# A second buffer for the sample values, raw w_out blocks in the space of the gate tiles, the w_out split shared with GpSimd, and sample jobs between the thirds of the last gate tile

## The chip, the cores and the metric

The kernel runs on one core of one Trainium2 chip. The metric is the device time of one execution in microseconds (us). The kernel before takes 933.46 us (median of 3 runs, 929.93 to 934.06).

## The reference, cut to what matters

One inference step of a one-layer decoder, for a prompt of 1024 tokens and for 8 sample sequences with one new token each and 512 past tokens in a paged cache (pages of 128 tokens).

```python
hn = rms_norm(x, g_n)
p  = hn @ w_in                  # 3344 columns: q, k, v of every group, and the gate path z
o_a = fox_attention(...)        # 4 heads, cumulative log-forget bias
o_b = nsa_attention(...)        # compressed blocks (64 tokens @ w1, w2), selected blocks, window
o_c = pool_mix(...)             # trailing means, per-group linear map
o_m = mem_attention(...)        # 256 memory tokens
y  = x + (concat[o_a, o_b, o_c, o_m] * silu(z)) @ w_out     # w_out 1024 x 1024
y  = rms_norm(y, final_g)
```

For the samples the past keys and values come page by page from `cache_fox_kv` and `cache_nsa_kv` by `page_table`, and from `state_nsa_win` and `cache_mem_kv`. Everything is float32.

## The kernel before, in words

**Engines and queues.** Five instruction streams are written out by hand and linked by semaphores: `pe` (TensorE), `act` (ScalarE), `dve` (VectorE), `pool` (GpSimd), `sp` (SyncE). Four of them walk the same list `STEPS`. Nearly all DMAs are issued by `sp`, in the order written, and a wait in that stream holds everything behind it. A page is found with `page(i)`, a load of a table entry into a register of `sp`.

**Products in two parts.** A float32 product is made of three passes (`passes`, L500 to L502): hi by hi, hi by lo and lo by hi, where hi is the operand rounded to fp32r and lo the rest. The projection weights come in 31 tiles of 128 columns (`TILES`); `pool` splits each one from `WR` into `WH` and `WL` (L1827, L1829), and `project(m)` multiplies it with the normalised tokens `hh`, `hl` (1032 columns: 1024 prompt tokens and 8 samples) in three thirds of 344.

**Compression.** `load_pair(q)` brings half of what a sample's page pair needs (32 values of q). For each of its two pages it issues one DMA for each of two heads g, 256 contiguous bytes at a time (L1937). `pair_job(n, kind)` on TensorE turns the four tiles of sample n with transposes (L658), and ScalarE or VectorE copies the result to `FT`. `compress(kind)` multiplies `FT` with `w1` in four quarters (L676); each quarter is a DMA of 1 MB (`load_w1`, L1944) into one of two halves of `PP`. On `sp` these DMAs stand among the pair loads: the fourth quarter of kind 0 is behind the loads of q = 23 and 24.

**Sample keys and values.** `sample_keys` runs four gate tiles in thirds and turns and scores the keys of one sample between thirds (L802, L811 to L817). It ends with small products for the new keys (L836 to L843). `sample_values` runs the last gate tile in three thirds (`project_chunk`), then turns the probabilities `X` (L854 to L858), then the pooled sums (L863), then multiplies these with the pool map (L869).

**Output product.** `mix` takes nine row tiles t: eight of 128 prompt rows and t = 8 with the 8 samples. Each has two halves of 512 columns, eight steps of k and three passes: 48 matmuls of 512 columns. From t = 1 on, `values(b)` stands ahead of a tile (L886): 14 products of the probabilities of sample b with its values. t = 1 has `values(0)` and `values(1)` ahead of it, t = 2 to 7 one sample each. Values are in the single ring `v_ring` (`XT` and three parts of `PP`), so the loads of sample b + 1 wait for the products of sample b (`load_values`, counted by `s_vr`).

**The raw w_out.** It comes in eight blocks of 128 columns (`load_wo`, L2118) into four places, two in `WR` and two in `PP`. ScalarE makes the hi part of each (`out_hi`) into the space of `hh`, VectorE the lo part (`out_lo`, L1487) into that of `hl`. Blocks 4 to 7 are loaded when the lo part of blocks 0 to 3 is done. Because the blocks overwrite columns of `hh`, block 0 and 1 can be written after the first third of the last gate tile, blocks 2 to 4 after the second, blocks 5 to 7 after the last.

**Gates.** `gate_product(n)` (L1473) multiplies the attention output by the tile `AUG[:, j]` of silu(z) and counts `s_zo`; after it that tile is only needed for the 8 sample columns. `gate_hi(t)` and `gate_lo(t)` split the product for a row tile. At the end of a row tile VectorE adds the input rows (L1798), ScalarE squares and takes the root, VectorE scales (L1777), and `sp` stores.

Of the kernel before, what the change touches and what calls it, by code (L numbers as in the profile page):

```python
# [21 lines left out]
F32 = mybir.dt.float32  # L22
# [7 lines left out]
P = 128  # L30
# [3 lines left out]
NB = 8  # L34
# [119 lines left out]
def build(nc, x_p, x_s, c_fox, c_lf, c_nsa, st_win, st_pool, c_mem, ptab, mem_p, norm_g, w_in, b_f, pe_, w1,  # L154
# [3 lines left out]
    with ExitStack() as ctx:  # L158
# [65 lines left out]
        gg = NAT[:, 0:KC * NB].rearrange("p (k b) -> p k b", k=KC)  # L224
# [45 lines left out]
        def pair_slot(q):  # L270
# [8 lines left out]
            return where.rearrange("p (a c) -> p a c", a=2)  # L279
# [63 lines left out]
        s_wo = [sem(f"s_wo{i}") for i in range(4)]  # L343
        s_woh = sem("s_woh")
        s_wol = sem("s_wol")
        s_eva = sem("s_eva")
# [37 lines left out]
        s_kv = [sem(f"s_kv{i}") for i in range(4)]  # L384
        s_lfp = sem("s_lfp")
# [60 lines left out]
        v_ring = [XT[:, 0:1024], PP[:, 2048:2560], PP[:, 2560:3072], PP[:, 3072:3584]]  # L446
        XW = WR[:, :, :, :].rearrange("p s k c -> p s (k c)")

        def wo_raw(j):

            if j % 4 < 2:
                return WR[:, (NT + j) % 2, :, :]
            return PP[:, (j % 2) * 1024:(j % 2 + 1) * 1024].rearrange("p (k c) -> p k c", k=KC)
# [6 lines left out]
        def _(pe):  # L460
# [386 lines left out]
            def sample_values():  # L847
                project_chunk(NT - 1, 0)
                project_chunk(NT - 1, 1)
                project_chunk(NT - 1, 2)  # L850
                pe.wait_ge(s_px, 1)
                out = job_a()
                for pg in range(NPG):
                    last = tr(out[:, pg * P:(pg + 1) * P], X[:, pg * P:(pg + 1) * P], ident[:, :])  # L854
                last.then_inc(s_TA, 1)
                out = job_d()
                tr(out[0:NB, 0:P], XN8[:, :], ident[:, :])
                tr(out[0:NB * SCB, P:P + 32], XC[0:32, 16:16 + NB * SCB], ident[0:32, 0:32]).then_inc(s_TD, 1)  # L858

# [4 lines left out]
                last.then_inc(s_TA, 1)  # L864
                jobs_taken()
# [5 lines left out]
                last.then_inc(s_TD, 1)  # L871

            def values(b):
# [6 lines left out]
                for pg in range(NPG):  # L880
                    for br, width, npg in ((0, 256, NPG), (1, P, NPG), (2, P, NPG), (3, 256, 2)):
                        if pg == 0:
                            pe.wait_ge(s_kv[br], (64 if br in (0, 1) else 16) * (NB + b + 1))
                        if pg >= npg:
                            continue
                        last = mm(PS[32 * br:32 * br + 32, 6 + p % 2, b % 2 * 256:b % 2 * 256 + width],  # L886
                                  PTs[:, pg, 32 * br:32 * br + 32], v_ring[br][:, pg * width:(pg + 1) * width],
# [1315 lines left out]
```

## Time and profile before

| | |
|---|---|
| time, median of 3 runs | 933.46 us (929.93 to 934.06) |
| time of the profiled execution | 932.5 us |
| its span, first to last instruction | 930.8 us |
| TensorE matmul busy | 826.7 us, 89% |
| VectorE, ScalarE, GpSimd busy | 42%, 29%, 16% |
| mean granted TensorE clock | 0.946 of full speed |

A line of the profile gives source line, engine, operation, names of output and inputs, and times in us. "SPq" is a DMA issue on SyncE. "PEclk" is the granted TensorE clock, 1.00 being 2.4 GHz and 0.50 being 1.2 GHz. A matmul is recorded longer than the step from one to the next, since consecutive ones overlap. An idle time is put down to whatever ended it.

### The profile page before, as it was taken

How to read it: one execution, taken by the hardware profiler on the slowest of the kernel's cores; microseconds unless marked ns; L12 is line 12 of the kernel's file. 1: busy time of each engine (PE TensorE's matmuls, PEld its weight loads, DVE VectorE, ACT ScalarE, POOL GpSimd, SP SyncE). 2: the span in 40 equal slices, each digit the busy share in tenths (PEclk: the TensorE clock that was granted, in tenths of full speed). 3: DMA queues.
4: the chain of work that ended last, by engine and by line, in shares of the span. 5: the costliest groups of instructions: out<-in, count | busy, mean ns of one | idle time of the engine just before them, and what ended most of it. 6: DMA issues, size and time to landing. Idle time of an engine off the chain costs nothing.

```text
span 930.8 us, 15434 instructions
## 1 busy us (share of the span) xinstructions
PE 826.7 (89%) x5755; PEld 679.0 (73%) x5755; DVE 395.4 (42%) x765; ACT 268.1 (29%) x624; POOL 146.2 (16%) x104
## 2 busy tenths in 40 slices
PE   3788998797999978899989999988999999799997
PEld 3788687794666978798956666668988788567773
DVE  3731734114565111206426777855833125433333
ACT  4612720103444102202125444631022224221111
POOL 4745001331000201103101000003231110000000
PEclk9979999897999989999799999989999999889999
DMA  7510002235321334040022000010135447365631
GB/s 227 171 49 24 1 22 47 57 77 156 105 113 30 103 103 133 21 136 23 14 84 62 2 1 2 1 26 25 47 87 159 146 134 193 93 198 186 204 103 49
DMA packets 110409, 79.45 MB, mean 85 GB/s; under 512 B 27237, under 2 KB 104308, under 8 KB 110264
## 3 DMA queue, kind: packets, MB, share of 16 engines
q1 hardware_dynamic: 108880, 77.66, 27.9%
q10 hardware_dynamic: 1456, 0.82, 0.4%
q8 instruction: 46, 0.75, 0.3%
q14 instruction: 27, 0.22, 0.1%
HBM read 68.81 MB, written 13.85 MB: 89 GB/s over the span
## 4 chain that ended last, share of the span: by engine, by line
PE 73%; DVE 10%; ACT 4%; issue 4%; DMA 4%; SPq 3%; POOL 1%; DVEq 0%; ACTq 0%; POOLq 0%
PE PS L500 14%; PE PS L502 14%; PE PS L501 14%; PE PS L582 6%; PE PS L628 5%; PE PS L607 4%; PE PS L676 3%; PE PS L802 2%; PE PS L886 2%; PE PS L592 2%; DVE AUG L1417 1%; DVE stat L1367 1%; PE PS L632 1%; DMA PP<-in_nsa_w 1%; PE PS L595 1%
## 5 line engine op out<-in xcount | busy, mean ns | idle before, releaser
L500 PE MATMUL PS<-HH,WH 128*128 128x344 f32 (+3 forms) x824 | 285.6, 347 | 7.2 <-issue 2.9
L501 PE MATMUL PS<-HL,WH 128*128 128x344 f32 (+3 forms) x824 | 280.1, 340 | 0.0
L502 PE MATMUL PS<-HH,WL 128*128 128x344 f32 (+3 forms) x824 | 279.8, 340 | 0.0
L500 PEld LDWEIGHTS PS<-HH,WH 128*128 128x128 f32 (+1 forms) x824 | 160.0, 194 | 21.4 <-issue 8.3
L501 PEld LDWEIGHTS PS<-HL,WH 128*128 128x128 f32 (+1 forms) x824 | 159.8, 194 | 7.9
L502 PEld LDWEIGHTS PS<-HH,WL 128*128 128x128 f32 (+1 forms) x824 | 159.5, 194 | 8.2
L1827 POOL TENSOR_TENSOR WH<-WR,onesc 128x1024 fp32r<-128x1024 f32 x31 | 61.3, 1977 | 604.2 <-PE PS L502 237.1
L1124 ACT ACTIVATE PP<-PS,stat 128x640 f32<-128x640 f32 (+7 forms) x96 | 67.8, 710 | 102.9 <-DVE stat L1367 102.9
L1367 DVE TENSOR_REDUCE stat<-PS 128x1 f32<-128x640 f32 (+7 forms) x96 | 65.1, 720 | 60.1 <-PE PS L595 59.7
L1829 POOL TENSOR_TENSOR WL<-WR,WH 128x1024 fp32r<-128x1024 f32 x31 | 78.2, 2522 | 2.4
L607 PE MATMUL PS<-ident,PP 128*128 128x128 f32 x472 | 67.6, 281 | 9.5 <-DVE AUG L1417 6.9
L607 PEld LDWEIGHTS PS<-ident,PP 128*128 128x128 f32 x472 | 54.9, 143 | 15.6 <-DVE AUG L1417 13.0
L582 PE MATMUL PS<-AUG 64*128 64x512 f32 (+3 forms) x288 | 59.9, 522 | 2.0 <-issue 2.0
L1417 DVE COPY AUG<-PS 128x512 f32<-128x512 f32 (+3 forms) x80 | 48.9, 628 | 8.3 <-PE PS L607 7.3
L628 PE MATMUL PS<-AUG,NAT 128*64 128x128 f32 (+1 forms) x640 | 47.2, 289 | 4.4 <-ACT AUG L1016 2.8
L676 PE MATMUL PS<-OB,PP 128*128 128x161 f32 x256 | 41.1, 326 | 10.2 <-DMA PP<-in_nsa_w 5.4
L676 PEld LDWEIGHTS PS<-OB,PP 128*128 128x128 f32 x256 | 39.9, 211 | 11.1 <-DMA PP<-in_nsa_w 6.1
L628 PEld LDWEIGHTS PS<-AUG,NAT 128*64 128x64 f32 x640 | 35.4, 136 | 11.2 <-DVE AUG L1417 4.2
L1016 ACT ACTIVATE AUG<-PS 128x128 f32<-128x128 f32 (+5 forms) x88 | 40.9, 465 | 7.7 <-PE PS L607 7.2
L1338 DVE COPY VS<-PS 64x8 f32<-64x8 f32 x8 | 1.4, 169 | 96.8 <-PE PS L502 96.8
L582 PEld LDWEIGHTS PS<-AUG 64*128 64x128 f32 x288 | 25.0, 193 | 22.0 <-issue 18.7
L1798 DVE TENSOR_TENSOR PP<-PS,WR 128x1024 f32<-128x1024 f32 (+1 forms) x9 | 11.0, 1223 | 66.3 <-PE PS L502 45.1
(322 smaller groups left out, 862.8 us busy)
## 6 DMA issues: line engine op xcount, KB each, us to landing
WR<-in_w_in SPq DMA_DIRECT2D x26, 512.0 KB, 4.3
PP<-in_nsa_w SPq DMA_DIRECT2D x8, 1024.0 KB, 6.1
OB<-in_x_prompt SPq DMA_DIRECT2D x8, 512.0 KB, 6.0
out<-NAT SPq DMA_DIRECT2D x2, 2048.0 KB, 7.8
PP<-in_cache_fox_kv SPq DMA_DIRECT2D x32, 128.0 KB, 2.3
PP<-in_cache_nsa_kv SPq DMA_DIRECT2D x64, 64.0 KB, 1.9
PP<-in_state_nsa_win SPq DMA_DIRECT2D x16, 256.0 KB, 3.0
PP<-in_cache_mem_kv SPq DMA_DIRECT2D x16, 256.0 KB, 3.2
```

The costliest lines, as they stand in the source:

```text
L500: mm(out, lhs[0], rhs[0], start=(k == 0), stop=False)
L501: mm(out, lhs[0], rhs[1], start=False, stop=False)
L502: return mm(out, lhs[1], rhs[0], start=False, stop=(k == KC - 1))
L582: mm(bk(score_bank(u, e) + c // 4)[:, 0:n * P], q[r, i * P:(i + 1) * P], k[r, (k0 + c) * P:(k0 + c + n) * P], start=True, stop=False)
L607: last = tr(bk(4 + g % 3)[:, (b - c) * P:(b - c + 1) * P], PP[:, p0:p0 + P], ident[:, :])
L628: mm(bk(7)[e * DH:(e + 1) * DH, 0:wide * P], v, p_, start=(b == 0), stop=(b == (1 if what == "mem" else nk - 1)))
L676: last = mm(bk(e)[:, 0:R_ALL + 1], w1s[:, n % 2, jj, e * P:(e + 1) * P], FT[:, j, :], start=(j == 0), stop=(j == NJ - 1))
L1124: last = act1(PP[:, c:c + nk * P], flat(score_bank(u, e), nk), ACT.Exp, bias=stat[:, k:k + 1], accum_out=stat[:, 16 + k:17 + k])
L1367: v.tensor_reduce(stat[:, k:k + 1], flat(score_bank(u, e), nk), AX.X, ALU.max, negate=True).then_inc(s_nm, 1)
L1417: v.tensor_copy(turned_p(u - 1, e, c, n), bk(4 + g % 3)[:, 0:n * P]).then_inc(s_cD, 1)
L1827: g.tensor_tensor(hi_, WR[:, s, :, :], ones, ALU.mult).then_inc(s_wcp, 1)
L1829: g.tensor_tensor(lo_, WR[:, s, :, :], hi_.bitcast(F32), ALU.subtract).then_inc(s_split, 1)
```

## The change

- **Pair loads.** Each page is fetched with one DMA for both heads (512 contiguous bytes), 64 issues instead of 128. `pair_job` makes eight matmuls with 64 weight columns, into one or the other half of the PSUM partitions, in place of four 128 x 128 transposes.
- **Values.** Two rings: even samples in `NAT` and `PP`, odd ones in the tiles `AUG[:, 0]` to `AUG[:, 2]`. Sample 1 is loaded first, then w_out blocks 0, 4, 5, 6, 2, 3, then three branches of sample 0, then blocks 1 and 7, then the last branch of sample 0.
- **w_out.** Blocks 4 to 7 go to `AUG[:, 3]` to `AUG[:, 6]` and wait only for a gate product. `pool` splits blocks 1, 3 and 5 with two tensor_tensor each; ScalarE and VectorE split the other five. The first half of row tile 0 waits for two blocks of each, the second half for all.
- **Order.** The pooled sums and the pool map stand ahead of the first and second third of the last gate tile, the probabilities between the second and the last. The copy of the pool map's result on VectorE stands ahead of the scaling of the probabilities.
- **Row tile 8.** hi and lo of the samples stand side by side in one weight tile (columns 0 to 7 and 32 to 39), so two matmuls do the work of three: 32 instead of 48. VectorE then adds two parts.

```diff
@@ pair_job (TensorE), load_pair (SyncE)
-                pe.wait_ge(s_pair[n], 128 * (kind + 1))
+                pe.wait_ge(s_pair[n], 64 * (kind + 1))
-                        last = tr(out[:, (2 * g + a) * P:(2 * g + a + 1) * P],
-                                  pair_slot(q)[:, g, :], ident[:, :])
+                        for r in range(2):
+                            last = mm(out[r * DH:(r + 1) * DH, (2 * g + a) * P:(2 * g + a + 1) * P],
+                                      pair_slot(q)[:, r, g * DH:(g + 1) * DH], ident[:, :], start=True, stop=True)
...
-                    for g in range(2):
-                        src = c_nsa[0, bass.ds(pg, 1), :, kind, g, :].rearrange("o (j r) d -> (o j) r d", r=2)
-                        sp.dma_start(dst, src).then_inc(s_pair[n], 16)
+                    src = c_nsa[0, bass.ds(pg, 1), :, kind, :, :].rearrange("o (j r) g d -> (o j) r (g d)", r=2)
+                    sp.dma_start(pair_slot(q)[a * DH:(a + 1) * DH], src).then_inc(s_pair[n], 16)
@@ places
-        v_ring = [XT[:, 0:1024], PP[:, 2048:2560], PP[:, 2560:3072], PP[:, 3072:3584]]
+        v_rings = [[NAT[:, 1024:2048], PP[:, 2048:2560], PP[:, 2560:3072], PP[:, 3072:3584]],
+                   [AUG[:, 0, 0:1024], AUG[:, 1, 0:512], AUG[:, 1, 512:1024], AUG[:, 2, 0:512]]]
...
+            return AUG[:, j - 1, 0:1024].rearrange("p (k c) -> p k c", k=KC)
+
+        WO_POOL = (1, 3, 5)
+        WO_CHUNK = (0, 0, 1, 1, 1, 2, 2, 2)
@@ mix (TensorE)
+                    if t == NQ:
+                        for half in range(2):
+                            for k in range(KC):
+                                c = slice(half * 512, (half + 1) * 512)
+                                both = TH[:, 1024 + k * P:1024 + k * P + 32 + NB]
+                                rest = both[:, 0:NB], wol[:, CHUNK[k], c]
...
-                            pe.wait_ge(s_wol, KC // 2 * (half + 1))
+                            pe.wait_ge(s_wol, 2 if half == 0 else 5)
+                            pe.wait_ge(s_wop, 2 if half == 0 else 3)
@@ end of the GpSimd stream
+            for n, j in enumerate(WO_POOL):
+                c = slice(j * P, (j + 1) * P)
+                pool.wait_ge(s_wo[j], 16)
+                if WO_CHUNK[j] < 2:
+                    pool.wait_ge(s_zp, 2 * (NT - 1 - ZK) + WO_CHUNK[j] + 1)
+                else:
+                    pool.wait_ge(s_proj, NT)
+                g.tensor_tensor(woh[:, :, c], wo_raw(j), ones, ALU.mult).then_inc(s_wph, 1)
+                pool.wait_ge(s_wph, n + 1)
+                g.tensor_tensor(wol[:, :, c], wo_raw(j), woh[:, :, c].bitcast(F32), ALU.subtract).then_inc(s_wop, 1)
@@ SyncE
-                    sp.wait_ge(s_wol, j - 3)
+                    sp.wait_ge(s_zo, j)
...
+            first = pages(1)
+            sp.wait_ge(s_zo, 3)
+            for br in range(4):
+                load_value(1, br, first)
             first = pages(0)
             load_wo(0)
+            for j in (4, 5, 6):
+                load_wo(j)
             load_wo(2)
             load_wo(3)
             for br in (1, 2, 3):
...
             load_wo(1)
+            load_wo(7)
-            sp.wait_ge(s_sx, 1)
-            load_kv(0, 0, 1, first, v_ring)
+            sp.wait_ge(s_sS, NB)
+            load_value(0, 0, first)
...
-                    sp.wait_ge(s_vr, 4 * (b - 1) + (2, 3, 4, 1)[br])
-                    load_kv(b, br, 1, pn, v_ring)
+                    sp.wait_ge(s_vr, 4 * (b - 2) + (2, 3, 4, 1)[br])
+                    load_value(b, br, pn)
@@ end of row tile 8 (VectorE)
+                            link(v.tensor_tensor(y1, y2[0:NB], XW[0:NB, s, :], ALU.add))
+                            last = v.tensor_tensor(y1, y2[32:32 + NB], y1, ALU.add)
```

## Rows read from the trace of the kernel before

**Rows 1.** The page: busy time of the engines, then two of its costliest groups
```profile
PE 826.7 (89%) x5755; PEld 679.0 (73%) x5755; DVE 395.4 (42%) x765; ACT 268.1 (29%) x624; POOL 146.2 (16%) x104
...
L1827 POOL TENSOR_TENSOR WH<-WR,onesc 128x1024 fp32r<-128x1024 f32 x31 | 61.3, 1977 | 604.2 <-PE PS L502 237.1
...
L1798 DVE TENSOR_TENSOR PP<-PS,WR 128x1024 f32<-128x1024 f32 (+1 forms) x9 | 11.0, 1223 | 66.3 <-PE PS L502 45.1
```
**Rows 2.** Waits of TensorE, whole span: sum, times, longest
```profile
PE PS L676 <- DMA PP<-in_nsa_w: 5.4, 3, 2.0
...
PE PS L500 <- POOL WL L1829: 2.2, 1, 2.2
```
**Rows 3.** Timeline, SyncE and TensorE, pairs of kind 0: start, duration
```profile
161.40 11.50 SPq L1937 DMA_DIRECT2D PP<-in_cache_nsa_kv  x12
...
170.57 1.09 PE L658 MATMUL PS<-ident,PP 128*128 128x128 f32 x4 [5.32 <-DMA PP<-in_cache_nsa_kv]
```
**Rows 4.** Timeline, SyncE and TensorE, compression of kind 0
```profile
336.49 7.44 SPq L1937 DMA_DIRECT2D NAT<-in_cache_nsa_kv  x8
343.98 0.59 SPq L1944 DMA_DIRECT2D PP<-in_nsa_w  x1
...
341.70 6.33 PE L676 MATMUL PS<-OB,PP 128*128 128x161 f32 x32 [2.00 <-DMA PP<-in_nsa_w]
350.00 4.65 PE L676 MATMUL PS<-OB,PP 128*128 128x161 f32 x32 [1.98 <-DMA PP<-in_nsa_w]
```
**Rows 5.** Windows: PE, PEld, DVE, ACT, POOL busy, PEclk, DMA share, GB/s
```profile
794.00:796.00 2.00, 1.69 (x10) 1.40 (x9) 1.21 (x6) 1.16 (x2) 0.00 (x0) 0.50 1.20 295
...
916.00:924.00 8.00, 8.00 (x36) 3.01 (x34) 1.40 (x2) 0.00 (x0) 0.00 (x0) 1.00 0.16 66
```
**Rows 6.** Timeline of TensorE from the last gate tile to row tile 1
```profile
788.91 0.60 PE L854 MATMUL PS<-ident,OB 128*128 128x128 f32 x4
...
794.64 0.77 PE L500 MATMUL PS<-HH,WH 128*128 128x512 f32 x1 [0.31 <-issue]
...
808.45 0.40 PE L886 MATMUL PS<-XT,NAT 128*32 128x256 f32 x1
...
820.81 0.50 PE L500 MATMUL PS<-HH,WH 128*128 128x512 f32 x1
```
**Rows 7.** Timeline of SyncE's DMA issues around w_out and the values
```profile
764.88 0.45 SPq L2108 DMA_DIRECT2D out<-OB  x1
768.22 0.39 SPq L2118 DMA_DIRECT2D WR<-in_w_out  x1
...
810.55 1.96 SPq L2059 DMA_DIRECT2D XT<-in_cache_fox_kv  x4
...
815.10 0.51 SPq L2065 DMA_DIRECT2D PP<-in_cache_mem_kv  x1
```
**Rows 8.** Timeline of ScalarE: hi parts of two w_out blocks as they land
```profile
794.09 1.06 ACT L1016 ACTIVATE HH<-WR 128x1024 fp32r<-128x1024 f32 x1 [1.10 <-DMA WR<-in_w_out]
...
797.67 1.06 ACT L1016 ACTIVATE HH<-PP 128x1024 fp32r<-128x1024 f32 x1 [0.71 <-DMA PP<-in_w_out]
```
**Rows 9.** DMA issues from 740 us on: count, KB, median us to landing
```profile
WR<-in_w_out SPq DMA_DIRECT2D x4, 512.0 KB, 4.5
```
**Rows 10.** Timelines of GpSimd and VectorE where both have two SBUF inputs
```profile
637.23 2.40 POOL L1829 TENSOR_TENSOR WL<-WR,WH 128x1024 fp32r<-128x1024 f32 x1
...
650.73 3.43 POOL L1829 TENSOR_TENSOR WL<-WR,WH 128x1024 fp32r<-128x1024 f32 x1
...
637.40 3.32 DVE L1430 TENSOR_TENSOR NAT<-PP 128x1038 f32<-128x1038 f32 x1
640.75 1.23 DVE L1430 TENSOR_TENSOR PP<-NAT 64x1036 f32<-64x1036 f32 x1
```
**Rows 11.** The chain that ended last: start, duration, matmuls of 64 and 32 columns
```profile
238.12 1.90 PE PS L628 x32
...
832.24 1.84 PE PS L886 x22
```

More of the change, by code:

```diff
@@ L342, in build @@
         s_zt = sem("s_zt")
-        s_wo = [sem(f"s_wo{i}") for i in range(4)]
+        s_wo = [sem(f"s_wo{i}") for i in range(KC)]
         s_woh = sem("s_woh")
         s_wol = sem("s_wol")
+        s_wop = sem("s_wop")
+        s_wph = sem("s_wph")
         s_eva = sem("s_eva")
@@ L384, in build @@
         s_kv = [sem(f"s_kv{i}") for i in range(4)]
+        s_kvo = [sem(f"s_kvo{i}") for i in range(4)]
         s_lfp = sem("s_lfp")
@@ L871, in sample_values @@
                 last.then_inc(s_TD, 1)
+                project_chunk(NT - 1, 1)
+                pe.wait_ge(s_px, 1)
+                out = job_a()
+                for pg in range(NPG):
+                    last = tr(out[:, pg * P:(pg + 1) * P], X[:, pg * P:(pg + 1) * P], ident[:, :])
+                last.then_inc(s_TA, 1)
+                mark["X"] = nA[0]
+                out = job_d()
+                tr(out[0:NB, 0:P], XN8[:, :], ident[:, :])
+                tr(out[0:NB * SCB, P:P + 32], XC[0:32, 16:16 + NB * SCB], ident[0:32, 0:32]).then_inc(s_TD, 1)
+                project_chunk(NT - 1, 2)
             def values(b):
@@ L919, in mix @@
                     s = t % 2
+                    if t == NQ:
[4 more added lines that the diff above has]
+                                rest = both[:, 0:NB], wol[:, CHUNK[k], c]
+                                if k == KC - 1:
+                                    mm(bk(half)[0:NB, :], *rest, start=False, stop=False)
+                                last = mm(bk(half)[0:32 + NB, :], both, woh[:, CHUNK[k], c], start=(k == 0),
+                                          stop=(k == KC - 1))
+                                if k < KC - 1:
+                                    mm(bk(half)[0:NB, :], *rest, start=False, stop=False)
+                        last.then_inc(s_y, 1)
+                        continue
                     for half in range(2):
                         if t == 0:
-                            pe.wait_ge(s_wol, KC // 2 * (half + 1))
+                            pe.wait_ge(s_wol, 2 if half == 0 else 5)
+                            pe.wait_ge(s_wop, 2 if half == 0 else 3)
                         if t == NB - 1 and half == 1:
@@ L927, in mix @@
                             c = slice(half * 512, (half + 1) * 512)
-                            out = bk(2 * s + half)[0:P if t < NQ else NB, :]
-                            last = passes(out, g, (woh[:, CHUNK[k], c], wol[:, CHUNK[k], c]), k)
+                            last = passes(bk(2 * s + half), g, (woh[:, CHUNK[k], c], wol[:, CHUNK[k], c]), k)
                     last.then_inc(s_y, 1)
@@ L1233, in _ @@
                 elif step == "sample_values":
-                    take_chunk(NT - 1, 0)
+                    out = job()
+                    done(copy(PLT.rearrange("p j b -> p (j b)"), out[:, 0:2 * NB]))
                     act.wait_ge(s_sx, 1)
@@ L1716, in _ @@
                     v.tensor_reduce(XC[0:32, 4:5], XC[0:32, 8:16], AX.X, ALU.max, negate=True).then_inc(s_sx, 1)
+                    out = job()
+                    done(v.tensor_copy(oTs[:, 6:8, :], out[:, 0:2 * NB].rearrange("p (j b) -> p j b", j=2)))
                     dve.wait_ge(s_se, 1)
@@ L1736, in _ @@
                     done(v.tensor_copy(PTc, out[0:NB * SCB, P:P + 32]))
-                    out = job()
-                    done(v.tensor_copy(oTs[:, 6:8, :], out[:, 0:2 * NB].rearrange("p (j b) -> p j b", j=2)))
+                    out_lo(4, 3)
+                    gate_product(9)
+                    out_lo(6, 4)
+                    out_lo(7, 5)
+                    gate_lo(1)
+                    dve.wait_ge(s_fA, mark["X"])
+                    dve.wait_ge(s_fD, nD[0])
                     for i in (6, 7):
@@ L2072, in _ @@
             for br in range(4):
[L2073 removed]
+                load_kv(0, br, 0, first, k_ring, s_kv)
             sp.wait_ge(s_lfr, 1)
@@ L2126, in _ @@
                     slot_read(NB - 1, max(br, 2))
-                load_kv(0, br, 1, first, v_ring)
+                load_value(0, br, first)
             load_wo(1)
-            sp.wait_ge(s_sx, 1)
-            load_kv(0, 0, 1, first, v_ring)
+            load_wo(7)
+            sp.wait_ge(s_sS, NB)
+            load_value(0, 0, first)
+            sp.wait_ge(s_sS, NB + 1)
             sp.dma_start(gf, fin_g.rearrange("(o d) -> o d", o=1).partition_broadcast(P)).then_inc(s_gf, 16)
-            for j in range(4, KC):
-                load_wo(j)
             def load_values(b):
```

109 lines of the change are left out of this document (52 added, 57 removed).

## The prediction

> **What bounds the kernel now.** First the page: TensorE is busy 89% of the span and no other engine half of it [rows 1]. So the path is TensorE's own list, and the change can gain in two ways only: fewer matmuls, or shorter holes between them. The waits of TensorE by what ended them come next [rows 2]. Two kinds are touched by the edits: waits for compression weights and cached pages, and one for a split by GpSimd. The timelines of SyncE and TensorE say why these came late [rows 3, 4]. Last come the stretch from the last gate tile to row tile 1 [rows 6] and the windows [rows 5]. The reader should see two holes there. Between the turned probabilities (788.91) and the first matmul of row tile 0 (794.64) only small sample jobs run, and the granted clock then is 0.50, that is 1.2 GHz; row tile 0 takes 808.45 - 794.64 = 13.81 us. Between 808.45 and 820.81 there are 12.36 us for two samples' values, whose products take 1.84 us each where nothing is late [rows 11]. The second sample's loads are issued at 810.55, when the ring is free [rows 7].
>
> **Pair loads.** TensorE first. Eight matmuls of 64 columns replace four transposes of 128. At full clock 32 such matmuls take 1.90 us [rows 11], so eight take 0.48; the four transposes took 1.09 at half clock [rows 3], 0.54 at full. I count nothing; with 16 jobs the ends are -1 and +1 us. Then SyncE. Four page look-ups fill the time from 764.88 + 0.45 to 768.22, 0.72 us each [rows 7]. Twelve issues with five look-ups between them took 11.50 [rows 3], so an issue costs (11.50 - 3.60) / 12 = 0.66. Half of the issues go.
>
> In kind 0 the job at 170.57 waited 5.32 us for q = 5, whose last issue stood behind seven issues and three look-ups: 161.40 + 6.78 = 168.2, so 2.4 us to land. Now three issues and three look-ups stand ahead: 161.40 + 4.14 + 2.4 = 167.9, 2.6 us sooner. The start at 161.40 hangs on a VectorE result (SyncE copies the forget biases just ahead) and stays. The wait of 2.2 us for GpSimd [rows 2] lies before it, on a weight load behind 16 pair issues, and should go too; but TensorE then only reaches the same late pages earlier. So the two together give 2.6, not 4.9.
>
> In compression the fourth quarter's weights were issued at 343.98 behind eight pair issues and waited for until 350.00 [rows 4], 6.0 us later. Four issues less (2.64) bring them at 347.4; TensorE is ready at 348.0, so the wait of 1.98 goes. The slot for them was free at 339.7, before the third quarter began to wait, and holds nothing back. The other waits in this group end with loads that wait for TensorE itself. **Sum: -4.6 us**; bounds -6 (clock regained as well) and 0 (if issue time per page grows with the wider rows).
>
> **w_out, values and the order of jobs.** The pooled sums and the map now precede the last gate tile's second third, so TensorE would be ready for row tile 0 at about 791 to 792, against 794.64. I ask when the split blocks are ready. SyncE is free at 765.3. It now looks up sample 1's pages (2.9, to 768.2), issues its ten loads (810.55 to 815.61 in rows 7, so 5.1, to 773.3), looks up sample 0's pages (2.9, to 776.2), and only then issues block 0, which went at 768.22 before. A block lands 4.5 us after its issue [rows 9], so block 0 at 780.7, early enough. But all the transfers now stand in one row. Blocks 5 and 7 landed so close behind each other that two blocks need 797.67 - 794.09 = 3.58 us, 1.79 each [rows 8], at the 295 GB/s of the window [rows 5]. Block 1 is the seventh block: six steps, 10.7 us, and 768 KB of values of sample 0 ahead of it, 2.7 us at the same rate. It lands at 780.7 + 13.4 = 794.1.
>
> GpSimd takes block 1 first. A block costs it 1.98 [rows 1] + 2.40 [rows 10] + small gaps, 4.4 us, so blocks 1 and 3 would be done at 802.9. Now the rows on sharing: VectorE's op at 637.40 took 3.32 instead of 1.23 and ended 1.1 us after GpSimd's, which began first; GpSimd's at 650.73 took 3.43 instead of 2.40 [rows 10]. The two take turns where both read two SBUF tensors. VectorE has lo parts of blocks 6 and 7 and of row tile 1 to do in just this stretch; I let two of the three fall into GpSimd's chain, at 1.03 each: 805.0 (bounds 802.9 and 806.0).
>
> The Trainium skill says the same against the change: GPSIMD Engine Reference, section Specifications, has the SBUF interfaces shared with VectorE, with contention where VectorE's instruction has two SBUF inputs. By it the sum would be that of 805 or 806, without it that of 803; the trace agrees, with 3.43 against 2.40 us.
>
> So row tile 0 starts at 805.0, 10.4 us later than before. What is queued behind: TensorE's whole mix, hence every later evict and store. GpSimd's third block ends at 809.5 to 811; the first half of tile 0 lasts from 805 to about 813 at its old speed, so that wait is hidden, and costs what it exceeds 813. Tile 0 takes the old 13.81 us, half clock at its head included: 818.8. All values are there by then (the last transfer, sample 0's fox part, lands near 798), so two samples take 3.7 us and 0.1: 822.6 against 820.81. **Sum: +1.8 us.** The hole of the values is filled, but its time has been moved to the front of row tile 0. Later samples are already hidden behind 11 us of matmuls in each tile and gain nothing. The eight small stores and the input rows follow on SyncE by about 798; the rows land before 806, long before 818.8 where VectorE wants them.
>
> **Row tile 8.** 36 matmuls start in 8.00 us [rows 5], 0.22 each; 16 less save 3.6. They end the kernel's list, so all of it is on the path. VectorE pays one more operation over 1024 columns behind them, 1.22 [rows 1] and a gap. **Sum: -2.35 us.** What comes next there, the store of tile 7 and the input row of the samples, is done by then.
>
> **Total:** -4.6 + 1.8 - 2.35 = -5.2 us. Against the profiled execution (932.5) that is 927.3; the median of the runs is 0.96 above it, 928.3. I take 928.
>
> **Rivals.** About 0.5% (4.7 us) is what a measurement of this kernel tells from no change: 928.8 and 938.1 are the bounds.
>
> 1. *The blocks come in time.* If block 1 landed by the end of the first third (782) and block 3's split needed only the second third (786.5), GpSimd would be done at 791, and the tile would start at 792 without a clock loss: 48 x 0.22 = 10.7 us, then 3.8: 806.5 against 820.8, -14 in place of +1.8, in all 911 to 912. For it: SyncE could be faster than its look-ups in rows 7 say, and the wait there may hide another cause. Against it: 3.9 MB between blocks 0 and 1 at 295 GB/s. Halfway cases lie at 917 to 924. Chance 0.2 for the two.
> 2. *The early gains are not kept, or GpSimd is later still.* If the wider pair loads cost SyncE more each, or all three VectorE operations and more meet GpSimd, then the total is between -3 and +4: 930 to 937. For it: each term rests on a difference of 2 to 3 us against landing times that vary as much. Chance 0.18.
> 3. *Slower, by one mechanism: the row of transfers.* The blocks and values between (3.9 MB) take 13.4 us at the rate of rows 5 and 8. A us more is a us on the path, so from 10.8 us more, a row 1.8 times as slow (163 GB/s), the total passes 938.1; at twice the time it is 927.3 + 13.4, 940.7. For it: six blocks in one row were never seen in this trace, only four at a time, and small pages are mixed in. Against it: the window that was full moved 295 GB/s. Chance 0.12.
> 4. *The second ring does nothing, all values were hidden anyway:* excluded by 12.36 us in rows 6 against 3.7.
>
> My forecast (924 to 932) has chance 0.5, of which 0.3 below 928.8. Faster: 0.3 + 0.2 = 0.5. Same: 0.2 + 0.18 = 0.38. Slower: 0.12. For 8 in 10 the range goes down into the halfway cases, 917, and up to 936; the likeliest case's own is 924 to 932.
>
> **What the changed profile would show.** The pair job near 170 waits under 5 us and its end comes at 168; no wait for weights at compression's fourth quarter. The first w_out issue is near 775 less the early gain, and TensorE stands idle some 13 us before row tile 0, released by GpSimd's lo part of block 3; GpSimd's first of six operations is released by a DMA. Between row tiles 0 and 1 there are 4 us, not 12. Row tile 8 takes 7.5 us, with two VectorE operations behind it. I am wrong if TensorE's wait before row tile 0 is short (blocks come faster than one in 1.79 us, or issued earlier), or if it is ended by VectorE or ScalarE; and if the pair jobs show issues longer than 0.66 us or matmuls slower than 0.06 each.

## The result and the profile after

| | before | after |
|---|---|---|
| median of 20 runs each | 931.69 us (926.35 to 939.45) | 925.52 us (920.54 to 930.92) |
| ratio, 95% interval | | 0.9932 (0.9911 to 0.9953) |
| profiled execution, its span | 932.5, 930.8 us | 924.19, 922.4 us |
| mean granted TensorE clock | 0.946 | 0.959 |

The change gains 0.7%, about 6.2 us of 931.7. The two profiled executions differ by 8.4 us. To see where, I cut both at starts of the same GpSimd instructions (the split of a projection tile, `WH<-WR`) and at the first matmuls of row tiles 0 and 1. Every run below is cut in the same way; no times of different kernels are compared on one clock. Line numbers are some 10 to 50 higher in the kernel after (L668 is the old L658, L686 the old L676, L509 to L511 the old L500 to L502).

| stretch, us | before | after | difference |
|---|---|---|---|
| start to the split at 89.85 | 89.85 | 89.69 | -0.2 |
| kind 0 pair loads and attention, to 311.87 | 222.02 | 218.07 | -3.9 |
| compression of kind 0, to 366.11 | 54.24 | 52.62 | -1.6 |
| kind 1 pair jobs, to 423.37 | 57.26 | 58.55 | +1.3 |
| code that no edit touches, to the last projection split (751.36) | 327.99 | 325.74 | -2.3 |
| from it to row tile 1 (820.81) | 69.45 | 70.26 | +0.8 |
| row tile 1 to the end of the span | 109.99 | 107.47 | -2.5 |

The fifth line is the one to distrust: nothing there was edited. Over all ten kernels profiled in this case the same code takes 324.5 to 333.9 us there, and its length follows the granted clock of the stretch: 324.5 to 326.2 us at a mean of 0.97 (three profiles, that of the kernel after among them), 328.0 to 329.7 at 0.96 (five, that of the kernel before among them), 332.3 and 333.9 at 0.95. So the profiled pair overstates the gain by some 2 us, and what remains, 6.1, is close to the 6.2 of the medians.

The page of the kernel after, engines' busy time; [rows 1] has the same line of before:

```profile
PE 815.7 (88%) x5931; PEld 674.2 (73%) x5931; DVE 396.2 (43%) x763; ACT 265.7 (29%) x621; POOL 160.9 (17%) x110
```

Waits of TensorE in the kernel after, by what ended them (sum, times, longest); compare [rows 2]:

```profile
PE PS L503 <- DVE OB L1324: 15.3, 7, 6.4
PE PS L509 <- POOL HL L1936: 15.0, 1, 15.0
...
PE PS L686 <- DMA PP<-in_nsa_w: 5.2, 3, 2.2
...
PE PS L668 <- DMA PP<-in_cache_nsa_kv: 4.1, 1, 4.1
```

One wait of 15.0 us for GpSimd is new, the longest of the kernel; the waits of compression for weights have hardly moved (5.4 to 5.2). Timelines of TensorE, kernel after: the late pair job and compression's third and fourth quarters ([rows 3, 4]), then the last third, row tile 0 and row tile 1 ([rows 6]):

```profile
166.62 1.97 PE L668 MATMUL PS<-ident,PP 128*64 128x128 f32 x16 [4.13 <-DMA PP<-in_cache_nsa_kv]
...
337.41 4.65 PE L686 MATMUL PS<-OB,PP 128*128 128x161 f32 x32 [1.60 <-DMA PP<-in_nsa_w]
344.27 4.65 PE L686 MATMUL PS<-OB,PP 128*128 128x161 f32 x32 [2.21 <-DMA PP<-in_nsa_w]
...
781.97 0.32 PE L511 MATMUL PS<-HH,WL 128*128 128x344 f32 x1
797.33 0.77 PE L509 MATMUL PS<-HH,WH 128*128 128x512 f32 x1 [15.04 <-POOL HL L1936]
...
811.36 0.40 PE L900 MATMUL PS<-NAT 128*32 128x256 f32 x1
...
814.93 0.50 PE L509 MATMUL PS<-HH,WH 128*128 128x512 f32 x1
```

The sample jobs no longer stand between the last third and row tile 0, and the products of two samples now take 814.93 - 811.36 = 3.57 us where they took 12.36. But in front of row tile 0 TensorE has nothing to do for 15 us. SyncE's issues and GpSimd's timeline say why:

```profile
757.38 0.44 SPq L2154 DMA_DIRECT2D out<-OB  x1
760.50 3.00 SPq L2105 DMA_DIRECT2D AUG<-in_cache_fox_kv  x4
...
768.84 0.37 SPq L2164 DMA_DIRECT2D WR<-in_w_out  x1
...
781.39 0.47 SPq L2164 DMA_DIRECT2D WR<-in_w_out  x1
```

```profile
786.75 1.89 POOL L1934 TENSOR_TENSOR HH<-WR,onesc 128x1024 fp32r<-128x1024 f32 x1 [37.71 <-DMA WR<-in_w_out]
788.73 2.35 POOL L1936 TENSOR_TENSOR HL<-WR,HH 128x1024 fp32r<-128x1024 f32 x1
791.03 2.87 POOL L1934 TENSOR_TENSOR HH<-PP,onesc 128x1024 fp32r<-128x1024 f32 x1
793.98 3.20 POOL L1936 TENSOR_TENSOR HL<-PP,HH 128x1024 fp32r<-128x1024 f32 x1
```

Block 0 of w_out is issued at 768.84, 11.0 us after SyncE was done with the store at 757.38 + 0.44; block 1 is issued at 781.39 and has landed at 786.75, 17.9 us behind block 0's issue. GpSimd needs 10.4 us for blocks 1 and 3, and its last two operations are longer than the 1.98 and 2.40 of [rows 1, 10]. Windows of the row of transfers, of the hole and of row tile 0, kernel after (columns as in [rows 5]):

```profile
769.00:787.00 18.00, 13.29 (x93) 12.45 (x90) 11.62 (x26) 10.56 (x16) 0.25 (x1) 0.98 0.98 276
```

```profile
782.00:797.00 15.00, 0.29 (x2) 0.00 (x1) 10.44 (x12) 4.29 (x6) 10.09 (x4) 0.64 0.78 248
797.00:804.00 7.00, 6.67 (x17) 5.31 (x18) 0.00 (x0) 0.00 (x0) 4.42 (x3) 0.55 0.00 0
804.00:811.00 7.00, 7.00 (x31) 5.65 (x31) 0.00 (x0) 0.00 (x0) 0.00 (x0) 1.00 0.01 2
```

From block 0's issue until block 1 is there the DMA engines are busy 98% of the time, so the transfers themselves are the row. The granted clock is at its lower level (1.2 GHz, 0.50) for most of the first six microseconds of row tile 0, as it was before; so the hole costs its own length and, behind it, a slow start of the tile. VectorE after the last row tile, kernel after:

```profile
914.73 1.21 DVE L1835 TENSOR_TENSOR PP<-PS,WR 8x1024 f32<-8x1024 f32 x1 [3.18 <-PE PS L941]
915.98 1.22 DVE L1836 TENSOR_TENSOR PP<-PS,PP 8x1024 f32<-8x1024 f32 x1
```

Row tile 8's first matmul starts at 907.11 and the sum can start at 914.73: 7.6 us.

### The profile page after: what moved, and what is told of

It reads as the page before. It is cut to its first block, busy times and chain, and to the rows that moved or that the text cites. A ratio compares the mean times of both kernels' runs of the same rounds, so it can differ in the third digit from the quotient of the medians.

```text
span 922.4 us, 15598 instructions
## 1 busy us (share of the span) xinstructions
PE 815.7 (88%) x5931; PEld 674.2 (73%) x5931; DVE 396.2 (43%) x763; ACT 265.7 (29%) x621; POOL 160.9 (17%) x110
## 4 chain that ended last, share of the span: by engine, by line
PE 71%; DVE 9%; SPq 5%; issue 4%; DMA 4%; ACT 4%; POOL 2%; DVEq 0%; POOLq 0%; ACTq 0%
PE PS L509 14%; PE PS L511 13%; PE PS L510 13%; PE PS L591 6%; PE PS L637 5%; PE PS L616 4%; PE PS L686 3%; PE PS L601 2%; SPq L2105 2%; PE PS L900 2%; DVE AUG L1445 1%; PE PS L812 1%; DVE stat L1395 1%; DMA PP<-in_nsa_w 1%; PE PS L668 1%
## 5 line engine op out<-in xcount | busy, mean ns | idle before, releaser
L509 PE MATMUL PS<-HH,WH 128*128 128x344 f32 (+2 forms) x808 | 276.7, 342 | 19.7 <-POOL HL L1936 15.0
L510 PE MATMUL PS<-HL,WH 128*128 128x344 f32 (+2 forms) x808 | 271.4, 336 | 0.0
L511 PE MATMUL PS<-HH,WL 128*128 128x344 f32 (+2 forms) x808 | 271.1, 335 | 0.0
L509 PEld LDWEIGHTS PS<-HH,WH 128*128 128x128 f32 x808 | 156.2, 193 | 32.2 <-issue 23.7
L511 PEld LDWEIGHTS PS<-HH,WL 128*128 128x128 f32 x808 | 156.1, 193 | 6.0
L510 PEld LDWEIGHTS PS<-HL,WH 128*128 128x128 f32 x808 | 156.3, 193 | 5.7
L686 PE MATMUL PS<-OB,PP 128*128 128x161 f32 x256 | 40.0, 320 | 9.8 <-DMA PP<-in_nsa_w 5.2
L686 PEld LDWEIGHTS PS<-OB,PP 128*128 128x128 f32 x256 | 38.8, 205 | 10.7 <-DMA PP<-in_nsa_w 6.0
L1285 ACT ACTIVATE WR<-PP 128x1024 f32<-128x1024 f32 (+1 forms) x9 | 9.5, 1058 | 100.5 <-DVE PP L1831 93.3
```

The lines of the kernel that those rows point to most:

```text
L509: mm(out, lhs[0], rhs[0], start=(k == 0), stop=False)
L510: mm(out, lhs[0], rhs[1], start=False, stop=False)
L511: return mm(out, lhs[1], rhs[0], start=False, stop=(k == KC - 1))
L686: last = mm(bk(e)[:, 0:R_ALL + 1], w1s[:, n % 2, jj, e * P:(e + 1) * P], FT[:, j, :], start=(j == 0), stop=(j == NJ - 1))
```

## Experiments

The kernel before ran beside each: 932.67 us (median of 35 runs) beside the first four experiments, which have 12 runs each, 932.14 us (11 runs) beside the last four, which have 6 runs each. So kernels of different groups are best compared by their ratios. "Hole" is the idle time of TensorE right before row tile 0. The last two columns count from the last projection split on GpSimd.

| kernel | median us | ratio to before (95%) | hole | row tile 0 starts | end |
|---|---|---|---|---|---|
| before, profiled | 931.69 | 1 | 0.3 | 43.3 | 179.4 |
| after, profiled | 925.52 | 0.9932 (0.9911 to 0.9953) | 15.0 | 52.7 | 177.7 |
| pair loads and matmuls alone | 925.82 | 0.9922 (0.9892 to 0.9951) | as before | 43.1 | 179.7 |
| eight matmuls alone | 934.91 | 0.9999 (0.9971 to 1.0026) | as before | 41.4 | 177.4 |
| row tile 8 alone | 930.92 | 0.9962 (0.9932 to 0.9991) | as before | 41.6 | 175.5 |
| sample 1's values late | 930.2 | 0.9967 (0.9935 to 0.9998) | 8.6 | 46.3 | 181.4 |
| block 1 second | 920.77 | 0.9873 (0.9831 to 0.9916) | 0.6 | 44.8 | 170.7 |
| all blocks first | 915.38 | 0.9855 (0.9803 to 0.9906) | 0.6 | 47.9 | 171.2 |
| no GpSimd | 916.59 | 0.9835 (0.9789 to 0.9881) | 5.7 | 44.9 | 169.0 |
| blocks first, no GpSimd | 911.63 | 0.9774 (0.9730 to 0.9817) | 0.6 | 39.7 | 162.2 |

### 1. Pair loads and their matmuls alone

```diff
-                pe.wait_ge(s_pair[n], 128 * (kind + 1))
+                pe.wait_ge(s_pair[n], 64 * (kind + 1))
...
-                        last = tr(out[:, (2 * g + a) * P:(2 * g + a + 1) * P], pair_slot(q)[:, g, :], ident[:, :])
+                        for r in range(2):
+                            last = mm(out[r * DH:(r + 1) * DH, (2 * g + a) * P:(2 * g + a + 1) * P],
+                                      pair_slot(q)[:, r, g * DH:(g + 1) * DH], ident[:, :], start=True, stop=True)
...
-                        src = c_nsa[0, bass.ds(pg, 1), :, kind, g, :].rearrange("o (j r) d -> (o j) r d", r=2)
...
+                    src = c_nsa[0, bass.ds(pg, 1), :, kind, :, :].rearrange("o (j r) g d -> (o j) r (g d)", r=2)
...
```

> The kernel before with the pair part alone: one DMA per page for both heads, and eight matmuls of 64 weight columns per pair job. Theory A, the prediction's: fewer issues bring two late loads sooner, -4.6 us at the start of the attention of the second phase and after compression of kind 0, and the eight matmuls cost nothing; -4.6 us in all. Theory B, from the profile after: a pair job now shows 1.09 us at full clock and 1.97 at half, where it showed 0.60 and 1.09, so 16 jobs cost 16 x 0.45 = 7 us more of TensorE, of which some lies in waits that shrink; then the part is worth between 0 and +3 us of loss, or less gain than 2 us.

Measured: 925.82 us, ratio 0.9922 (0.9892 to 0.9951). The interval is -4.6 to -10 us and excludes that the early gain is lost. In the profiles, the time from the split at 89.85 to that at 423.37 is 333.5, 333.6 and 334.2 us in the three kernels with narrow loads, and 327.5 to 329.6 in the seven with wide ones, mean 329.1, against 333.8: **-4.7 us**, with -3.6 in kind 0, -2.8 in compression and +1.6 in the kind 1 jobs. The +1.6 is a cost of the eight matmuls, as experiment 2 shows.

### 2. The eight matmuls alone, loads as before

```diff
-                        last = tr(out[:, (2 * g + a) * P:(2 * g + a + 1) * P], pair_slot(q)[:, g, :], ident[:, :])
+                        for r in range(2):
+                            last = mm(out[r * DH:(r + 1) * DH, (2 * g + a) * P:(2 * g + a + 1) * P],
+                                      pair_slot(q)[:, g, r * DH:(r + 1) * DH], ident[:, :], start=True, stop=True)
```

> The kernel before with its narrow loads (two DMAs per page), but eight matmuls of 64 weight columns per pair job in place of four transposes. Theory A: matmuls into two halves of the partitions overlap as in the attention's products, no change (within 1 us). Theory B: 0.45 us more per job, 16 jobs, less what the job waiting for a DMA hides: +5 to +7 us.

Measured: 934.91 us, ratio 0.9999 (0.9971 to 1.0026): no cost that the medians can tell (the interval is -2.7 to +2.4 us). Yet the operation is not the one that I had costed. Two jobs of kind 1, kernel with the eight matmuls alone, timeline of TensorE:

```profile
369.12 1.97 PE L659 MATMUL PS<-ident,VW 128*64 128x128 f32 x32 [1.06 <-ACT KCs L1017]
371.42 1.97 PE L659 MATMUL PS<-ident,NAT 128*64 128x128 f32 x32 [0.34 <-ACT OB L1017]
```

and the same place in the kernel before:

```profile
367.67 1.09 PE L658 MATMUL PS<-ident,VW 128*128 128x128 f32 x8 [1.06 <-ACT KCs L1016]
369.50 1.57 PE L658 MATMUL PS<-ident,NAT 128*128 128x128 f32 x8 [0.74 <-ACT OB L1016]
```

Each line covers two jobs, so 16 of the new matmuls leave 32 records. Each leaves two. The page confirms it: 5931 - 5755 = 176 records more = 16 jobs x (16 - 4) - 16 in row tile 8. It is not the 64 columns: compression issues 128 float32 matmuls with 128 weight columns over its two kinds and leaves 256 records (L676 in its page), while a transpose leaves one (64 of them at L658 in the kernel before, 64 records). What changed is that transposes became plain float32 matmuls. Two jobs take 1.97 us in place of 1.09. The second line shows what hides half of it: the wait for ScalarE's copy shrinks from 0.74 to 0.34 us, so from the first line to the second it is 2.30 us instead of 1.83. Sixteen jobs make some 4 us at that rate if none waits for pages or copies.

In kind 1 the profiles show it. TensorE's first two quarters of compression of kind 1, in the kernels of experiment 3 (old transposes), of experiment 2 and in the kernel after:

```profile
391.70 10.68 PE L676 MATMUL PS<-OB,PP 128*128 128x161 f32 x64 [1.15 <-DVE OB L1581]
```

```profile
393.42 9.01 PE L677 MATMUL PS<-OB,PP 128*128 128x161 f32 x64 [1.08 <-DVE OB L1567]
```

```profile
386.24 10.68 PE L686 MATMUL PS<-OB,PP 128*128 128x161 f32 x64 [1.11 <-DVE OB L1593]
```

The split of the projection tile ahead of the jobs starts at 367.90, 367.56 and 360.38 in the three, so compression starts 23.80, 25.86 and 25.86 us behind it. It is 25.9 in all eight kernels with the new matmuls, all at full clock up to there, as that of experiment 3 is; in the kernel before it is 24.96, with the granted clock at 0.50 for a part of the jobs. So the eight jobs of kind 1 cost 2.1 us. The kernel of experiment 2 wins 1.7 back behind them, since it alone has the full clock in the first quarter (the two quarters take 9.01 us in place of 10.68). That is why its whole stretch is no longer than that of the kernel before (56.75 and 57.26), and why the kernels with wide loads and the same matmuls need 58.4.

### 3. The new row tile 8 alone

```diff
+                    if t == NQ:
+                        for half in range(2):
+                            for k in range(KC):
...
+                                both = TH[:, 1024 + k * P:1024 + k * P + 32 + NB]
+                                rest = both[:, 0:NB], wol[:, CHUNK[k], c]
...
+                            link(v.tensor_tensor(y1, y2[0:NB], XW[0:NB, s, :], ALU.add))
+                            last = v.tensor_tensor(y1, y2[32:32 + NB], y1, ALU.add)
...
```

> The kernel before with the new row tile 8 alone (two matmuls in place of three, and two adds on VectorE). Prediction: 16 x 0.23 = 3.6 us less of TensorE at the end of the list, 1.25 us more of VectorE behind it, -2.35 us. Rival: the samples' gate product or the store of tile 7 ends later than row tile 8 now starts or ends, so nothing is gained (0 us). The profile shows the last matmul to the end as 6.9 + 1.25 us if the first holds.

Measured: 930.92 us, ratio 0.9962 (0.9932 to 0.9991), -3.5 us with an interval of -0.8 to -6.3 that holds the -2.35. VectorE after its last scaling of row tile 7, first the kernel with this edit:

```profile
926.02 1.21 DVE L1819 TENSOR_TENSOR PP<-PS,WR 8x1024 f32<-8x1024 f32 x1 [3.18 <-PE PS L928]
927.27 1.22 DVE L1820 TENSOR_TENSOR PP<-PS,PP 8x1024 f32<-8x1024 f32 x1
```

then the kernel before:

```profile
924.31 1.21 DVE L1798 TENSOR_TENSOR PP<-PS,WR 8x1024 f32<-8x1024 f32 x1 [6.88 <-PE PS L502]
```

VectorE waits 3.70 us less and pays 1.25 for the second sum: -2.45. That the profiled span was longer than that of before (933.7) is no cost of the edit: its clock was 0.933, and the untouched stretch alone took 333.9 us.

### 4. The kernel after with sample 1's values loaded late

```diff
-            first = pages(1)
-            sp.wait_ge(s_zo, 3)
-            for br in range(4):
-                load_value(1, br, first)
             first = pages(0)
             load_wo(0)
...
+            pn = pages(1)
+            for br in range(4):
+                sp.wait_ge(s_vr, (2, 3, 4, 1)[br])
+                load_value(1, br, pn)
```

> The kernel after with sample 1's values loaded where the kernel before loads them, after sample 0's products: the second ring is not used for what it is for, and look-ups and ten issues are taken from ahead of w_out. Theory A (the prediction's): the start of row tile 0 is set by the row of transfers and GpSimd behind it, so it comes 8 us sooner (block 0 issued 8 us sooner), and the wait for sample 1's values comes back with 8 to 9 us; the total is that of the kernel after within 1.5 us. Rival: GpSimd alone sets the start (its blocks are slow whatever lands when), then the start does not move, and the total is 8 us above the kernel after.

Measured: 930.2 us, ratio 0.9967 (0.9935 to 0.9998), 3.3 us above the kernel after by the two ratios. GpSimd gets block 1 35.3 us after the last split, 6.8 sooner than in the kernel after, and row tile 0 starts 6.4 sooner. So SyncE's look-ups, issues and the transfer of sample 1 cost 6.4 to 6.8 us of the path where they stand. But the wait behind row tile 0 comes back: from the first product of values (809.68) to row tile 1 (822.55) it is 12.9 us where the kernel after takes 3.6. The balance at row tile 1 is +2.5 us. The expectation, 8 us in front and 8 to 9 behind with a total within 1.5 us, was too high for the front. By the profiles the second ring pays for itself (the intervals of the two ratios overlap), but it gives 6.4 of the 9.3 us back in front of row tile 0.

### 5. Block 1 issued second

```diff
-            for j in (4, 5, 6):
+            for j in (0, 1, 3, 2, 4, 5, 6):
                 load_wo(j)
-            load_wo(2)
-            load_wo(3)
...
-            load_wo(1)
```

> The kernel after with one thing changed: the issue order of the w_out blocks is 0, 1, 3, 2, 4, 5, 6, then the values, then 7. Theory A: the 15.0 us hole ahead of row tile 0 is the row of transfers in front of block 1; block 1 now lands some 12 us sooner, GpSimd starts as soon as the first third is done and ends block 3 about 7.5 us after the second third, so the hole shrinks from 15 to 3 us and the total falls by 11 to 13 us against the kernel after. Rival B: GpSimd is the bound (two blocks of 5.2 us each with VectorE's turns between), with more turns now that VectorE works beside it all the time: the hole shrinks by 5 us or less.

Measured: 920.77 us, ratio 0.9873 (0.9831 to 0.9916). Waits of TensorE, this kernel:

```profile
PE PS L875 <- DVE cs L1754: 3.4, 1, 3.4
...
PE PS L509 <- POOL HL L1936: 3.2, 1, 3.2
```

The 15.0 us are gone; the 3.2 stand in the middle of row tile 0 (at 802.78), where the second half wants GpSimd's third block. Row tile 0 starts 7.8 us sooner, not 15, and by the two ratios the total falls by 5.5 us, where 11 to 13 (or, by the rival, 5 or less) were expected: neither theory had the whole. The last third ends 6.7 us later than in the kernel after. Of that, 3.4 is a new wait in front of it, for VectorE's softmax of the samples, which was in time in the kernel after. The other 3.3 is the granted clock. It is at 0.50 behind that wait, in part of the last third, and in part of the first third, which costs 1.5 us in this kernel and in the three that follow; why it fell there no run shows. The next run shows the cause of the wait best. GpSimd's third block suffers from the other side, timelines of GpSimd and VectorE in this kernel:

```profile
793.34 6.87 POOL L1934 TENSOR_TENSOR HH<-AUG,onesc 128x1024 fp32r<-128x1024 f32 x1 [2.78 <-PE PS L511]
```

```profile
797.25 1.21 DVE L1509 TENSOR_TENSOR WL<-OB,WH 128x1024 fp32r<-128x1024 f32 x1
```

The operation that takes 1.89 us elsewhere took 6.87. VectorE ran five operations with two SBUF inputs back to back, from 793.43 to 797.25 + 1.21 = 798.46, and GpSimd's ended 1.75 us behind the last of them: it was held through all five, though it is recorded as begun before the first.

### 6. All blocks but one ahead of sample 1's values

```diff
+            for j in (0, 1, 4, 5, 6, 3, 2):
+                load_wo(j)
             first = pages(1)
             sp.wait_ge(s_zo, 3)
...
+            load_wo(7)
             first = pages(0)
-            load_wo(0)
-            for j in (4, 5, 6):
-                load_wo(j)
...
```

> The kernel after with SyncE's order 0, 1, 4, 5, 6, 3, 2 of the w_out blocks ahead of the page look-ups and loads of sample 1, then block 7, then sample 0. Theory A: as with block 1 second, -12 us against the kernel after; blocks come even earlier than they can be used, so there is nothing above that, within 2 us; values of both samples land before 793 and are not waited for (needed at about 797). Rival: the values now come late and a wait stands between row tiles 0 and 1 again (some us back).

Measured: 915.38 us, ratio 0.9855 (0.9803 to 0.9906). Against the kernel after that is 7.2 us by the ratios, where 12 were expected; its six runs lie apart (914.2 to 925.0), and the intervals of experiments 5, 6 and 7 overlap, so what follows rests on the profiles. The rival's wait between row tiles 0 and 1 did not come: 3.6 us as in the kernel after. Row tile 0 starts later than with experiment 5 (47.9 against 44.8). GpSimd, then VectorE, in this kernel:

```profile
772.38 1.90 POOL L1934 TENSOR_TENSOR HH<-WR,onesc 128x1024 fp32r<-128x1024 f32 x1 [26.01 <-PE PS L511]
774.35 2.39 POOL L1936 TENSOR_TENSOR HL<-WR,HH 128x1024 fp32r<-128x1024 f32 x1
776.69 2.07 POOL L1934 TENSOR_TENSOR HH<-PP,onesc 128x1024 fp32r<-128x1024 f32 x1
778.85 2.34 POOL L1936 TENSOR_TENSOR HL<-PP,HH 128x1024 fp32r<-128x1024 f32 x1
```

```profile
772.86 1.43 DVE L1748 TENSOR_TENSOR cs<-cs,GC 128x1 f32<-128x1 f32 x1
774.32 2.70 DVE L1749 TENSOR_SCALAR OB<-OB,cs 128x513 f32<-128x513 f32 x1
777.06 1.74 DVE L1750 TENSOR_SCALAR cs<-E,OB 128x8 f32<-128x8 f32 x1
...
778.89 2.31 DVE L1752 TENSOR_TENSOR cs<-cs,GC 32x1 f32<-32x1 f32 x1
```

and the same four operations of VectorE in the kernel after, where GpSimd is idle:

```profile
773.99 0.16 DVE L1748 TENSOR_TENSOR cs<-cs,GC 128x1 f32<-128x1 f32 x1
774.18 0.49 DVE L1749 TENSOR_SCALAR OB<-OB,cs 128x513 f32<-128x513 f32 x1
774.71 0.23 DVE L1750 TENSOR_SCALAR cs<-E,OB 128x8 f32<-128x8 f32 x1
...
775.03 0.15 DVE L1752 TENSOR_TENSOR cs<-cs,GC 32x1 f32<-32x1 f32 x1
```

Four operations of 1.03 us together take 8.18. Read the ends: each ends within 0.3 us of the GpSimd operation beside it (774.29 and 774.28, 777.02 and 776.74, 778.80 and 778.76, 781.20 and 781.19). A column of one element waits as long as a tile of 1024. TensorE waits 5.2 us for the result, and then runs the last third (783.20 to 789.36) at a mean granted clock of 0.62.

The Trainium skill (GPSIMD Engine Reference, section Specifications) has the SBUF interfaces shared with VectorE, with contention where VectorE's instruction is in a 2-port performance mode or has two SBUF inputs. The trace agrees for the two inputs; that two TENSOR_SCALARs here wait as well would come under the other half of that rule, if they run in such a mode, which no row here names.

### 7. The transfers of the kernel after, GpSimd left out of the split

```diff
-            for n, j in enumerate(WO_POOL):
...
-                g.tensor_tensor(woh[:, :, c], wo_raw(j), ones, ALU.mult).then_inc(s_wph, 1)
...
+                    out_hi(3)
+                    for j in (5, 6, 1, 7):
+                        out_hi(j)
...
-                            pe.wait_ge(s_wol, 2 if half == 0 else 5)
-                            pe.wait_ge(s_wop, 2 if half == 0 else 3)
+                            pe.wait_ge(s_wol, 7 if half == 0 else 8)
...
```

ScalarE makes all eight hi parts and VectorE all eight lo parts; block 1 is the seventh of them, so the first half of row tile 0 waits for seven lo parts.

> The kernel after with its order of transfers, but ScalarE and VectorE split all eight blocks (in the order 0, 2, 4, 3, 5, 6, 1, 7). Theory A, the row of transfers: block 1 still lands at 786.7 (in the profile's time), its hi and lo parts take 2.3 us, so row tile 0 starts at about 789 in place of 797.3: -8 us. So of the hole of 15 us, GpSimd's two blocks are 10.6 and the transfers 4.4 to 7. Rival: VectorE and ScalarE become the bound (eight blocks of 1.1 us each and gates), start not before 793, -4 us.

Measured: 916.59 us, ratio 0.9835 (0.9789 to 0.9881). Waits of TensorE, this kernel:

```profile
PE PS L509 <- DVE HL L1515: 5.7, 1, 5.7
```

The order of the transfers is that of the kernel after, and block 1 lands at the same place, 42.1 us after the last split. Yet of the hole of 15.0 us only 5.7 is left. **GpSimd's share of it is about 9 us, the row of transfers' about 6** (by the start of row tile 0 it is 7.8 and, down to experiment 8, 5.2, since the last third ends 1.5 us later in both, by the slow first third that experiment 5 has too). ScalarE and VectorE split a block in 1.06 and 1.2 us in two steps that overlap from block to block, where GpSimd takes over 4 for each, one after the other.

### 8. Both: blocks first, GpSimd left out

The edits of 6 and 7 together, blocks 5, 6 and 7 split last.

> The kernel after with all w_out blocks but 7 issued ahead of the values, and ScalarE and VectorE splitting all eight in the order of their numbers, no work on GpSimd. Theory A: no transfer and no shared interface is left; row tile 0 starts about 1 us after the last third (783 in the profile's time), -14 us against the kernel after, 1 to 2 us better than with GpSimd. Rival: VectorE's eight lo parts are too slow between the thirds, so that sharing with GpSimd pays (this one 2 us or more slower than all blocks first with GpSimd).

Measured: **911.63 us, ratio 0.9774 (0.9730 to 0.9817)**, 20.5 us below the kernel before and 13.9 below the kernel after (21.1 and 14.7 by the ratios). Row tile 0 of this kernel, timeline of TensorE, and a window around it:

```profile
788.86 0.50 PE L509 MATMUL PS<-HH,WH 128*128 128x512 f32 x1 [0.55 <-ACT AUG L1123]
```

```profile
787.00:800.00 13.00, 12.45 (x57) 9.96 (x55) 8.71 (x14) 4.72 (x6) 0.00 (x0) 1.00 0.65 211
```

The wait left is the one for the last tile's silu. Against the kernel after, row tile 0 starts 12.9 us sooner, and it takes 11.4 us rather than 14.0, since without a hole the granted clock stays at 1.00. The two make 15.5, and the whole from the last split to the end is 15.6 us shorter.

## Why the prediction was right

The forecast was 928, with -5.2 us as the sum; the medians give -6.2, the profile without its untouched stretch -6.1. It was right in its total and near in every term, but several of its reasons were not, and in the pair loads errors of opposite sign cancel. Step by step:

- **Pair loads, -4.6: measured -4.3 in the profiled pair, -4.7 over all profiles.** That the sum is so close is luck: kind 0 and compression gave 1.8 more than their 4.6 over all profiles, and the kind 1 jobs took 1.6 of it back. In kind 0 I had 2.6 and the stretch gave 3.9. The late job's wait ended at 166.62, not at 167.9. Six issues with five look-ups took 7.20 us (160.15 to 167.35), near the 7.56 of my 0.66 and 0.72; what I missed lies ahead of them. I wrote that SyncE's start at 161.40 "stays"; it came 1.25 us sooner. VectorE's scaling of the forget biases, one step of that chain, ran beside a GpSimd lo part in the kernel before (149.38 to 151.73; first row below, kernel before) and alone in the kernel after, where that split had begun at 140.60 (second row), 1.05 us for the one operation:

```profile
150.54 1.73 DVE L1554 TENSOR_SCALAR OB<-OB 4x1024 f32<-4x1024 f32 x1
```

```profile
150.35 0.68 DVE L1581 TENSOR_SCALAR OB<-OB 4x1024 f32<-4x1024 f32 x1
```

- **Compression, -2.0 as a wait that goes: measured -1.6, and the wait did not go.** The fourth quarter's issue did move, from 2.3 us behind the start of the third quarter's matmuls to 0.1 behind it (337.54 against 337.41). But the transfer landed 6.7 us after its issue rather than 6.0, so the fourth quarter starts 8.30 - 6.86 = 1.4 us sooner after the third, not 2.0. And the third quarter now ran at full clock, 4.65 in place of 6.33 us, so TensorE was ready earlier and waits 2.21 us where it waited 1.98. The clock is not what gave the 1.4: the fourth quarter starts when its weights land in both kernels. With the third quarter at 6.33 us in the kernel of experiment 6 the distance is 7.08 us; it is 6.6 to 7.1 in the seven kernels with wide loads and 8.2 to 9.1 in the three with narrow ones.
- **Eight matmuls, 0: no cost in the medians, 2.1 us in the traces of kind 1.** "At full clock 32 such matmuls take 1.90 us, so eight take 0.48" read records as matmuls. Eight take about 0.98, and 16 jobs at that price are outside the end of +1 us that I gave. The jobs of kind 1 alone cost 2.1 us against transposes at full clock (experiment 2), and 0.9 against the kernel before, whose transposes ran partly at 0.50. What those of kind 0 cost isn't shown; they stand beside page waits and copies. The kind 1 stretch, where I had 0, shows +1.3.
- **w_out and values, +1.8: measured +0.8.** Counted from the last split: block 0's issue 24.8 predicted, 24.2 measured; block 1 there at 42.7, 42.1; row tile 0 at 53.6, 52.7; its length 13.8, 14.0; the two samples 3.8, 3.6. GpSimd's two blocks took 10.4, between my reckonings without and with two collisions (8.8 and 10.9). Block 1 landed 17.9 us after block 0's issue, which is my 4.5 + 13.4. The steps stand; the hole is 15 and not 13 because TensorE was through with the thirds 37.6 after the split, where I had about 40. This part never ran by itself. By the ratios alone it would cost more: experiments 1 and 3 make -7.3 and -3.5 us, the kernel after -6.3, which leaves +4.5 us, give or take 4.4. One reading was loose: I put the clock between 788.91 and 794.64 at 0.50, but its mean there is 0.88; it is at 0.50 where row tile 0 begins.
- **Row tile 8, -2.35: measured -2.45** in VectorE's wait and second sum, -2.5 in the stretch.

Of the rivals, that the blocks come in time was excluded by the order of the issues: with the blocks first, experiment 6 has them in time and gives 915.38 us, experiment 8, which leaves GpSimd out as well, 911.63. That this is the rival's figure (911 to 912) is chance, since the rival left the split on GpSimd. That the early gains are not kept fell with experiment 1. The slow row of transfers fell with the 276 GB/s between 769 and 787. The runs add what the prediction had not priced apart: the row of transfers is the smaller part of the hole, GpSimd's serial work the larger.

## What to carry to other kernels

A share for a third engine is worth its slowest chain, not its sum of work: here GpSimd took three of eight blocks from two engines that had time to spare, cost 9 us of the total, and held VectorE's small operations as soon as the blocks came early enough (experiments 5 and 6). Order the transfers by who needs them first and by who is slowest at working on them; the second ring saved 9 us of waiting behind row tile 0, but its loads, in front of the weights, gave 6 of them back. To attribute a gain of less than 1%, cut the trace at the same instructions in both kernels, and treat any difference in untouched code as the noise of the method. Here that noise was the granted clock; a part that seems to cost nothing can hide behind it.

## What the runs showed of the hardware

- **A VectorE operation of one column can take as long as a GpSimd operation over 1024.** 128x1 and 32x1 went from 0.16 and 0.15 us to 1.43 and 2.31, and a TENSOR_SCALAR over 128x513 from 0.49 to 2.70, beside GpSimd splits. It goes the other way too: 6.87 us for 1.89, through five VectorE operations back to back.
- **A plain float32 matmul leaves two records, a float32 transpose one.** Two pair jobs of eight matmuls with 64 weight columns take 1.97 us at full clock, where two of four 128-column transposes take 1.09.
- **The same code with the same inputs takes 324.5 to 333.9 us** in ten profiled executions, and the time goes with the mean granted clock of the stretch: 0.97 for the shortest, 0.95 for the longest. One profile of each kernel can't show a gain of a few microseconds unless it is read by place.
